# Modulation with stationary weights and two moving columns, most of it placed in slots of phase one

## The chip, the core and the metric
One NeuronCore of a Trainium2 chip. The time is that of the device for one execution, in microseconds (us). TensorE multiplies, VectorE and ScalarE work element by element, GpSimd builds masks, SyncE and ScalarE issue the transfers.

## What is computed
One step of a layer of a streaming encoder: 2048 prompt tokens and 64 sample tokens of width 1024, in float32. Cut to what the change touches:

```python
mod = jax.nn.silu(c) @ w_ada + b_ada              # c: (1, 1024), w_ada: (1024, 6144)
sh1, sc1, g1, sh2, sc2, g2 = jnp.split(mod[:, None, :], 6, axis=-1)
hn = rmsnorm(x, ln1_g) * (1.0 + sc1) + sh1
z = hn @ w_in                                     # four head groups read z
...
x = x + g1 * mix                                  # mix: concat of heads @ w_out
h2 = rmsnorm(x, ln2_g) * (1.0 + sc2) + sh2
x = x + g2 * (jnp.square(jax.nn.relu(h2 @ mlp_w1)) @ mlp_w2)
```

There are two vectors c, one for the prompt and one for the sample. Only sh1 and sc1 are needed before the input projection; the other four parts are read in the output projection and the MLP.

## The kernel before, in words
Three phases stand one after the other, each a block of its own with a join of all engines between them: `setup_phase` (the opening), `front_phase` (phase one: input projection and heads) and `tail_phase` (attention of later blocks, output projection, MLP). Features lie on the 128 partitions in KT = 8 tiles, tokens in the free dimension, in blocks of 512 (the first has the 64 sample tokens too, 576).

The opening computes the whole modulation in 12 chunks of 512 columns (NCH). For each, 2 MB of w_ada go into one of four `wada` buffers, issued by SyncE and ScalarE in turns. `chunk(c)` (L449 to L456) has c as the stationary side, 4 columns (`cful`, `chl`), and w_ada as the moving side: half of the depth in full float32, half as high and low parts, for which `halves_hi` (ScalarE, L272) and `halves_lo` (VectorE, L337) split the weights. The result is four rows in `pr`; `take_row` (L342) copies them, `turn_row` (L443) turns them into columns in `pm`, and `modulation(part)` on VectorE (L368 to L372) adds the bias and makes gs1 and gs2. Between the chunks lie the transposes of raw x (`turn("raw", f)`, stored to x_scratch), the squares and inverse roots, the transposes of normalised x (`xn`), which are evacuated into hT with scale gs1 and shift sh1 (L355), and the high and low parts hn_hi (L329) and hn_lo (L415).

Phase one walks slots. A block has 23 (SLOTS): slot 0 the low-rank strip, slots 1 to 22 one strip of 128 columns of w_in each. `strip(slot)` does 8 x 3 matmuls (high by high, low by high, high by low) for each column group of the block; block 0 has two groups of 288 columns. Its weights come by `load_weights` on SyncE (two slots ahead, into two buffers, after `w_lo_ok` of the strip two earlier), `weights_hi` on ScalarE (L864) and `weights_lo` on VectorE (L1089). Results go to a ring of four PSUM banks (`ring_no`, `bank_for`), which ScalarE empties in `ring_out`. Beside the strips a slot does the jobs that its number gives it (gates, norms, transposes, state updates, attention). The order on each engine is written out by hand in `step(slot)`; each engine works its list in order, so a wait in SyncE's list holds all its later loads and stores.

## Time and profile before
| | before |
|---|---|
| three plain runs, us | 2826.13, 2823.44, 2823.38 (median 2823.44) |
| the profiled execution, us | 2821.06 |
| its span, us | 2819.3 |
| TensorE busy | 96% (2718.6 us) |
| VectorE, ScalarE busy | 52%, 38% |
| moved | 485.99 MB, mean 172 GB/s |

The span runs from the first to the last instruction; the profiled execution has 1.8 us around it. Busy shares are means over phases with different limits, so they say what is scarce over the run and not what ends a stage.

### The profile page before, as it was taken

The page shows a single profiled execution, that of the slowest core. Times are in us where ns is not written, and L with a number is a line of the kernel's source. Part 1 is how long each engine was busy: PE and PEld are TensorE (multiplying, and loading weights), DVE is VectorE, ACT ScalarE, POOL GpSimd, SP SyncE. Part 2 cuts the span into 40 slices and gives each one's busy share as a digit, 9 for nine tenths or more (in the row PEclk, how much of TensorE's full clock was granted, in tenths as well). Part 3 has the DMA queues.
Part 4 walks back from the last instruction along what each step waited for, and adds up shares of the span by engine and source line. Part 5 has one row for each costly group of instructions (what it writes and reads, how often), then busy time and mean ns, then how long its engine had stood idle before and what let it go on. Part 6 is the DMA issues. An engine that isn't in the chain of part 4 may idle for free.

```text
span 2819.3 us, 36506 instructions
## 1 busy us (share of the span) xinstructions
PE 2718.6 (96%) x14669; PEld 2224.5 (79%) x14669; DVE 1459.5 (52%) x2315; ACT 1075.1 (38%) x1728; POOL 33.2 (1%) x43
## 2 busy tenths in 40 slices
PE   7999999999978999999999999999999999999996
PEld 2589777777766777777787878777777788999996
DVE  4455563554436657665564455555545434544553
ACT  3374846656434343433433322343222322221112
POOL 0000000000000000000000000001000000100000
PEclk9999999999989999999999999999999999999999
DMA  9533435324386676775435454534453643454441
GB/s 338 174 105 114 115 113 153 113 83 135 101 282 244 221 243 227 238 253 206 147 138 192 179 185 164 191 127 172 151 204 140 216 180 135 165 177 166 166 179 64
DMA packets 285934, 485.99 MB, mean 172 GB/s; under 512 B 21963, under 2 KB 168326, under 8 KB 285766
## 3 DMA queue, kind: packets, MB, share of 16 engines
q1 hardware_dynamic: 279526, 471.07, 48.7%
q10 hardware_dynamic: 6240, 12.58, 1.2%
q8 instruction: 118, 1.93, 0.3%
q14 instruction: 50, 0.41, 0.0%
HBM read 374.52 MB, written 109.06 MB: 172 GB/s over the span
## 4 chain that ended last, share of the span: by engine, by line
PE 62%; DVE 5%; ACT 2%; DMA 2%; issue 1%; SPq 1%; DVEq 0%; ACTq 0%
PE t_dn L2400 10%; PE t_dn L2404 10%; PE t_dn L2401 10%; PE t_dn L2442 7%; PE t_dn L2444 7%; PE t_dn L2443 7%; PE t_ob L2340 3%; PE t_sc L2317 2%; PE t_wt L2329 2%; DVE t_left L2137 1%; PE t_dn L2465 1%; PE t_dn L2467 1%; PE t_dn L2466 1%; DVE t_xs L2220 1%; DMA ring_lo<-lo_scratch 1%
## 5 line engine op out<-in xcount | busy, mean ns | idle before, releaser
L2400 PE MATMUL t_dn<-t_h_hi,ring_hi 128*128 128x512 f32 (+2 forms) x1600 | 588.0, 368 | 18.0 <-ACT t_h_hi L2027 7.1
L2220 DVE SCALAR_TENSOR_TENSOR t_xs<-t_dn,modT,t_xs 128x512 f32<-128x512 f32 (+2 forms) x768 | 422.5, 580 | 312.9 <-PE t_dn L2444 167.6
L2404 PE MATMUL t_dn<-t_h_lo,ring_hi 128*128 128x512 f32 (+2 forms) x1600 | 568.9, 356 | 3.8 <-DVE t_h_lo L2202 3.4
L2401 PE MATMUL t_dn<-t_h_hi,ring_lo 128*128 128x512 f32 (+2 forms) x1600 | 566.6, 354 | 0.0
L2442 PE MATMUL t_dn<-t_g_hi,t_w2h 128*128 128x512 f32 (+2 forms) x1120 | 412.3, 368 | 11.5 <-DVE t_xs L2220 9.3
L2444 PE MATMUL t_dn<-t_g_lo,t_w2h 128*128 128x512 f32 (+2 forms) x1120 | 396.6, 354 | 0.0
L2443 PE MATMUL t_dn<-t_g_hi,t_w2l 128*128 128x512 f32 (+2 forms) x1120 | 395.7, 353 | 0.0
L2252 DVE TENSOR_TENSOR t_rt<-t_rt 128x512 f32<-128x512 f32 (+2 forms) x160 | 95.8, 599 | 551.1 <-ACT t_g_hi L2076 551.1
L2400 PEld LDWEIGHTS t_dn<-t_h_hi,ring_hi 128*128 128x128 f32 x1600 | 304.2, 190 | 75.3 <-issue 32.1
L2404 PEld LDWEIGHTS t_dn<-t_h_lo,ring_hi 128*128 128x128 f32 x1600 | 303.3, 190 | 47.8 <-DVE t_h_lo L2202 6.9
L2401 PEld LDWEIGHTS t_dn<-t_h_hi,ring_lo 128*128 128x128 f32 x1600 | 304.5, 190 | 31.4 <-issue 0.5
L2074 ACT ACTIVATE t_rt<-t_dn 128x512 f32<-128x512 f32 (+2 forms) x160 | 83.7, 523 | 639.5 <-PE t_dn L2404 639.5
L1447 PE MATMUL f_zr<-hn_hi,ring_hi 128*128 128x512 f32 (+1 forms) x880 | 319.3, 363 | 6.5 <-ACT f_gb L897 2.6
L1449 PE MATMUL f_zr<-hn_hi,ring_lo 128*128 128x512 f32 (+1 forms) x880 | 309.9, 352 | 0.0
L1448 PE MATMUL f_zr<-hn_lo,ring_hi 128*128 128x512 f32 (+1 forms) x880 | 309.4, 352 | 0.0
L2442 PEld LDWEIGHTS t_dn<-t_g_hi,t_w2h 128*128 128x128 f32 x1120 | 211.9, 189 | 53.4 <-DVE t_xs L2220 20.6
L2444 PEld LDWEIGHTS t_dn<-t_g_lo,t_w2h 128*128 128x128 f32 x1120 | 211.7, 189 | 28.0
L1956 ACT ACTIVATE t_aT<-t_wt 128x512 f32<-128x512 f32 (+4 forms) x152 | 80.2, 528 | 398.9 <-PE t_wt L2329 398.8
L2443 PEld LDWEIGHTS t_dn<-t_g_hi,t_w2l 128*128 128x128 f32 x1120 | 212.3, 190 | 20.6
L1089 DVE TENSOR_TENSOR ring_lo<-f_wraw,ring_hi 128x1024 fp32r<-128x1024 f32 x90 | 110.1, 1224 | 215.8 <-ACT ring_hi L864 215.6
L1447 PEld LDWEIGHTS f_zr<-hn_hi,ring_hi 128*128 128x128 f32 x880 | 165.2, 188 | 39.4 <-issue 12.9
L864 ACT ACTIVATE ring_hi<-f_wraw 128x1024 fp32r<-128x1024 f32 x90 | 94.9, 1055 | 240.1 <-PE f_zr L1449 215.7
(344 smaller groups left out, 3426.1 us busy)
## 6 DMA issues: line engine op xcount, KB each, us to landing
ring_hi<-hi_scratch SPq DMA_DIRECT2D x120, 512.0 KB, 4.0
ring_lo<-lo_scratch SPq DMA_DIRECT2D x120, 512.0 KB, 4.9
t_w2h<-hi_scratch SPq DMA_DIRECT2D x96, 512.0 KB, 6.1
t_w2l<-lo_scratch SPq DMA_DIRECT2D x96, 512.0 KB, 7.1
f_wraw<-in_w_in_dram SPq DMA_DIRECT2D x88, 512.0 KB, 3.9
t_raw<-in_mlp_w_dram SPq DMA_DIRECT2D x64, 512.0 KB, 4.7
hi_scratch<-ring_hi SPq DMA_DIRECT2D x40, 512.0 KB, 5.6
lo_scratch<-ring_lo SPq DMA_DIRECT2D x40, 512.0 KB, 6.3
```

The source lines that it names most:

```text
L1089: dve.tensor_tensor(w_lo[n % 2][:, :, :], wraw[n % 2][:, :, :], w_hi[n % 2][:, :, :].bitcast(F32), ALU.subtract).then_inc(w_lo_ok, 1)
L1447: pe.matmul(out, wh, hi, start=(k == 0), stop=False)
L1448: pe.matmul(out, wh, lo, start=False, stop=False)
L1449: ins = pe.matmul(out, wl, hi, start=False, stop=(k == KT - 1))
L2220: ins = dve.scalar_tensor_tensor(out=cols, in0=dn[u % 4][:, s - a:t - a], scalar=modT[:, mod + f, m:m + 1], in1=cols, op0=ALU.mult, op1=AL ...
L2252: dve.tensor_tensor(r, r, r, ALU.mult).then_inc(g_sq, 1)
L2400: pe.matmul(out, hi[:, k, :], h_hi[:, k, a:e], start=(i == 0), stop=False)
L2401: pe.matmul(out, lo[:, k, :], h_hi[:, k, a:e], start=False, stop=False)
L2404: ins = pe.matmul(out, hi[:, k, :], h_lo[:, k, a:e], start=False, stop=(i == KT - 1))
L2442: pe.matmul(out[:, 0:e - a], hi[:, d, :], g_hi[c % 2][:, ft, a:e], start=(ft == 0), stop=False)
L2443: pe.matmul(out[:, 0:e - a], lo[:, d, :], g_hi[c % 2][:, ft, a:e], start=False, stop=False)
L2444: ins = pe.matmul(out[:, 0:e - a], hi[:, d, :], g_lo[c % 2][:, ft, a:e], start=False, stop=(ft == 1))
```

## The change
The opening computes only shift and scale of norm one, in 4 groups (PARTS) of 256 columns each of the two. Now the weights are the stationary side, 128x128 in float32 at a time, and the two vectors c are the moving side with 2 columns; results come out as columns on the partitions, so high and low parts, row copies and the small transposes are gone. The raw transposes of x stand ahead of the groups, the transposes of normalised x behind groups 1, 2 and 3, and the sample's in a PSUM bank of their own. Odd xn tiles are evacuated by ScalarE. All eight pieces of w_ada have buffers of their own and are loaded without waits; x comes first on ScalarE's queue in two halves. The opening also loads and splits the weights of strips 1 and 2 (EARLY).

The other 32 tiles of 128 columns are done in 16 groups of two, one at the end of each of slots 2 to 17 of phase one: SyncE loads two pieces of 512 KB into buffers not used yet (kst, oA, kq, tok), after TensorE is through with the group two earlier; TensorE does 2 x 8 matmuls with 2 columns into a bank of the ring; ScalarE adds the bias. VectorE makes gs2 in slot 20.

```diff
--- before.py
+++ after.py
...
 M_SH1, M_SC1, M_G1, M_SH2, M_SC2, M_G2 = 0, 8, 16, 24, 32, 40
+EARLY = 2
...
@@ -124,17 +125,14 @@
...
-    CT = CH // P
-    RING = 4
-    FIRST = 2 * D_MODEL // CH
-    HALF_K = KT // 2
+    PARTS = 4
+    PW = D_MODEL // PARTS
+    PF = KT // PARTS
     WIDE = BLK + DEC
 
...
@@ -149,47 +147,43 @@
...
+        wada = [[sb(f"wada{g}_{i}", [P, KT, PW]) for i in range(2)] for g in range(PARTS)]
+        early = [sb(f"early{n}", [P, KT, P]) for n in range(EARLY)]
...
+        def load_wada(eng, g, i):
+            col = (M_SH1, M_SC1)[i] * P + g * PW
+            eng.dma_start(wada[g][i][:, :, :], wa_v[:, :, col:col + PW]).then_inc(wada_in[g], 16)
...
@@ -206,30 +200,28 @@
...
-                    sp.dma_start(x_v[:, :, 0:BLK], raw[:, :, 0:BLK]).then_inc(raw_stored, 16)
-                    sp.dma_start(x_v[:, :, SEQ:SEQ + DEC], raw[:, :, BLK:WIDE]).then_inc(raw_stored, 16)
-
+            sp.dma_start(xsam[:, :], x_sample[0]).then_inc(xs_in, 16)
+            load_wada(sp, 0, 1)
+            load_rows(rows2, parts2, rows_in[1])
+            load_wada(sp, 1, 1)
+            for n in range(EARLY):
+                col = STRIPS_IN[n][2]
+                sp.dma_start(early[n][:, :, :], win_v[:, :, col:col + P]).then_inc(early_in, 16)
+            sp.dma_start(lra_raw[:, :].rearrange("p (k n) -> p k n", n=RANK), win_v[:, :, OFF_LRA:OFF_LRA + RANK]).then_inc(early_in, 16)
+            for g in range(2, PARTS):
+                load_wada(sp, g, 1)
+            for i in range(2):
+                sp.dma_start(mixc["wa2"][RANK * i:RANK * i + RANK, :], gla_wa2[0]).then_inc(blocks_in, 16)
+            sp.wait_ge(zeroed, 1)
+            for n in range(4):
+                for g, w in enumerate((rg_wa, rg_wx)):
+                    sp.dma_start(mixc["rgw"][64 * (n % 2):64 * (n % 2) + 64, g, n // 2,
+                                             64 * (n % 2):64 * (n % 2) + 64], w[0, n]).then_inc(blocks_in, 16)
+            for f in range(KT):
+                freed(sp, "raw", f)
+            freed(sp, "raws", 0)
+            sp.dma_start(x_v[:, :, 0:BLK], raw[:, :, 0:BLK]).then_inc(raw_stored, 16)
+            sp.dma_start(x_v[:, :, SEQ:SEQ + DEC], raw[:, :, BLK:WIDE]).then_inc(raw_stored, 16)
             sp.wait_ge(blocks_in, 16 * 10)
...
@@ -266,12 +257,9 @@
...
+            def early_halves(n):
+                act.wait_ge(early_in, 16 * (EARLY + 1))
+                act.activation(const["ring_hi"][:, n, :, :], early[n][:, :, :], ACT.Copy).then_inc(early_hi, 1)
...
@@ -283,24 +271,33 @@
...
-
-            for c in range(0, RING, 2):
-                load_wada(act, c)
+                    act.wait_ge(gs_ok, f // PF + 1)
...
+            def high(f):
+                freed(act, "xn", f)
+                act.wait_ge(s_ok, f + 1)
+                act.activation(hn_hi[:, f, :], hT[:, f, :], ACT.Copy).then_inc(hi_ok, 1)
+
+            for h in range(2):
+                act.dma_start(xrow[:, 2 * h:2 * h + 2, :], x_prompt[0, 2 * h * P:(2 * h + 2) * P, :].rearrange("(i p) n -> p i n", p=P)
+                              ).then_inc(x_in[h], 16)
+            for g in range(PARTS):
+                load_wada(act, g, 0)
...
@@ -309,37 +306,34 @@
...
+            for g in range(PARTS):
+                if g < EARLY:
+                    early_halves(g)
+                if g == 2:
+                    act.activation(mixc["lra_hl"][:, :, 0:RANK], lra_raw[:, :].rearrange("p (k n) -> p k n", n=RANK), ACT.Copy).then_inc(early_hi, 1)
+                    act.wait_ge(prm, 2)
+                    chain.link(act.activation(lam[:, 0, :], const["prm2"][:, R2_LAM:R2_LAM + 2], ACT.Abs))
+                    chain.link(act.activation(lam[:, 1, :], lam[:, 0, :], ACT.Exp, scale=-1.0))
+                    act.activation(lam[:, 2, :], lam[:, 1, :], ACT.Ln, bias=1.0).then_inc(lam_a, 1)
+                for f in range(g * PF + 1, (g + 1) * PF, 2):
+                    turned("xn", f)
+                for f in range(g * PF, (g + 1) * PF):
+                    high(f)
 
...
         def _(dve):
             chain = Chain(dve, dve_chain)
 
...
+            def early_rest(n):
+                dve.wait_ge(early_hi, n + 1)
+                dve.tensor_tensor(const["ring_lo"][:, n, :, :], early[n][:, :, :], const["ring_hi"][:, n, :, :].bitcast(F32), ALU.subtract)
+
+            def low(f):
+                dve.wait_ge(hi_ok, f + 1)
+                dve.tensor_tensor(hn_lo[:, f, :], hT[:, f, :], hn_hi[:, f, :].bitcast(F32), ALU.subtract)
 
...
@@ -351,70 +345,63 @@
...
+            def modulation(g):
+                dve.wait_ge(mod_full, g + 1)
+                a = g * PF
+                for i, m in enumerate((M_SH1, M_SC1)):
+                    out = modT[:, m + a:m + a + PF, :]
+                    ins = dve.tensor_tensor(out, pm[g % 2][:, i, :, :],
+                                            const["prm1"][:, R1_BADA + m + a:R1_BADA + m + a + PF].rearrange("p (f c) -> p f c", c=1)
+                                            .to_broadcast([P, PF, 2]), ALU.add)
+                    chain.link(ins)
+                ins = dve.scalar_tensor_tensor(
+                    out=gs1[:, a:a + PF, :], in0=modT[:, M_SC1 + a:M_SC1 + a + PF, :], scalar=1.0,
+                    in1=const["prm2"][:, R2_LN1 + a:R2_LN1 + a + PF].rearrange("p (f c) -> p f c", c=1).to_broadcast([P, PF, 2]),
+                    op0=ALU.add, op1=ALU.mult)
+                ins.then_inc(gs_ok, 1)
+                dve.wait_ge(gs_ok, g + 1)
+
+            def sample_columns(f):
+                dve.wait_ge(s_full, 1)
+                dve.tensor_scalar(hT[:, f, BLK:WIDE], ts[:, f, :], gs1[:, f, 1:2], modT[:, M_SH1 + f, 1:2],
+                                  ALU.mult, ALU.add).then_inc(s_ok, 1)
 
             turned("rows", 0)
-            dve.wait_ge(c_hi, 1)
...
+            for g in range(PARTS):
+                modulation(g)
+                for f in range(g * PF, (g + 1) * PF, 2):
+                    turned("xn", f)
+                for f in range(g * PF, (g + 1) * PF):
+                    sample_columns(f)
+                if g < EARLY:
+                    early_rest(g)
+                if g == 2:
+                    dve.wait_ge(early_hi, EARLY + 1)
                     dve.tensor_tensor(mixc["lra_hl"][:, :, RANK:], lra_raw[:, :].rearrange("p (k n) -> p k n", n=RANK),
                                       mixc["lra_hl"][:, :, 0:RANK].bitcast(F32), ALU.subtract)
-                if c == 4:
                     chain.link(dve.tensor_scalar(lam[:, 3, :], const["prm2"][:, R2_LAM:R2_LAM + 2], -1.0, 0.0,
...
@@ -436,53 +423,41 @@
...
-            def turn_row(c):
...
-            def chunk(c):
-                pe.wait_ge(wada_in[c % RING], 16 * (c // RING + 1))
-                wait(pe, row_read, c - 1)
-                for k in range(HALF_K):
-                    pe.matmul(pr[c % 2][:, :], cful[:, k, :], wada[c % RING][:, k, :], start=(k == 0), stop=False)
-                pe.wait_ge(wada_lo_ok, c + 1)
-                for k in range(HALF_K):
-                    pe.matmul(pr[c % 2][:, :], chl[:, HALF_K + k, :], wada_hi[c % 2][:, k, :], start=False, stop=False)
-                    ins = pe.matmul(pr[c % 2][:, :], chl[:, HALF_K + k, :], wada_lo[c % 2][:, k, :], start=False,
-                                    stop=(k == HALF_K - 1))
-                ins.then_inc(row_full, 1)
+            def modulation(g):
+                pe.wait_ge(wada_in[g], 32)
+                wait(pe, gs_ok, g - 1)
+                for i in range(2):
+                    for j in range(PF):
+                        for k in range(KT):
+                            ins = pe.matmul(pm[g % 2][:, i, j, :], wada[g][i][:, k, j * P:(j + 1) * P], cful[:, k, :],
+                                            start=(k == 0), stop=(k == KT - 1))
+                ins.then_inc(mod_full, 1)
...
             pe.wait_ge(masks, 2)
             turn("rows", 0)
+            pe.wait_ge(x_in[0], 16)
+            pe.wait_ge(x_in[1], 16)
+            for f in range(KT):
+                turn("raw", f)
+            pe.wait_ge(xs_in, 16)
+            turn("raws", 0)
+            turn("rows", 1)
             pe.wait_ge(silu_c, 1)
-            pe.wait_ge(c_lo, 1)
...
+            for g in range(2):
+                modulation(g)
+            pe.wait_ge(xn_ok, TPB + 1)
+            for k in range(KT):
+                ins = pe.transpose(ts[:, k, :], xsam[:, k * P:(k + 1) * P], ident[0:DEC, 0:DEC])
+            ins.then_inc(s_full, 1)
+            for f in range(2 * PF):
+                turn("xn", f)
+            for g in range(2, PARTS):
+                modulation(g)
+                for f in range(g * PF, (g + 1) * PF):
+                    turn("xn", f)
+
...
@@ -707,9 +693,16 @@
         def _(sp):
             def load_weights(slot):
                 n, i = weight_no(slot), slot % SLOTS
-                wait(sp, w_lo_ok, n - 1)
+                wait(sp, w_lo_ok, n - 1 - EARLY)
                 src, col = (wout_v, i * P) if slot >= NBLK * SLOTS else (win_v, STRIPS_IN[i - 1][2])
                 sp.dma_start(wraw[n % 2][:, :, :], src[:, :, col:col + P]).then_inc(w_in_sem[n % 2], 16)
+
+            def load_mods(g):
+                if g > 1:
+                    sp.wait_ge(z_full, ring_no["m", g - 2, 0] + 1)
+                for s in range(2):
+                    col = (16 + 2 * g + s) * P
+                    sp.dma_start(mod_w[g % 2][s], wada_v[:, :, col:col + P]).then_inc(mod_in[g % 2], 16)
 
...
@@ -754,8 +747,7 @@
             def load_kq(j):
                 sp.wait_ge(k_placed[0], 16)
                 sp.wait_ge(q_placed[0], 16)
-                if j:
-                    sp.wait_ge(z_full, ring_no["as", TPB - 1, 1] + 1)
+                sp.wait_ge(z_full, (ring_no["as", TPB - 1, 1] if j else ring_no["m", MODS - 1, 0]) + 1)
...
             def step(slot):
-                if slot and has_weights(slot + 2):
+                if slot > EARLY and has_weights(slot + 2):
                     load_weights(slot + 2)
+                if 2 <= slot < MODS:
+                    load_mods(slot)
...
@@ -816,8 +810,10 @@
...
-            load_weights(1)
-            load_weights(2)
+            load_weights(EARLY + 1)
+            load_weights(EARLY + 2)
+            load_mods(0)
+            load_mods(1)
             sp.wait_ge(init_ok, 1)
...
@@ -1020,6 +1016,14 @@
                 if kind == "nC" and j == 0:
                     norm_root(flows[0], "C")
 
+            def modulation(g):
+                bank = full("m", g, 0)
+                for s in range(2):
+                    m = 16 + 2 * g + s
+                    ins = act.activation(modT[:, m, :], bank[:, 2 * s:2 * s + 2], ACT.Identity,
+                                         bias=const["prm1"][:, R1_BADA + m:R1_BADA + m + 1])
+                ins.then_inc(z_free, 1)
+
...
@@ -1406,6 +1418,15 @@
                 if kind == "nC" and j == 0:
                     norm(flows[0], "C")
 
+            def modulation(g):
+                bank = bank_for("m", g, 0)
+                pe.wait_ge(mod_in[g % 2], 32 * (g // 2 + 1))
+                for s in range(2):
+                    for k in range(KT):
+                        ins = pe.matmul(bank[:, 2 * s:2 * s + 2], mod_w[g % 2][s][:, k, :], const["cful"][:, k, :],
+                                        start=(k == 0), stop=(k == KT - 1))
+                ins.then_inc(z_full, 1)
+
...
@@ -1429,8 +1450,8 @@
                 b, i = divmod(slot, SLOTS)
                 if i:
                     n = weight_no(slot)
-                    pe.wait_ge(w_hi_ok, n + 1)
-                    pe.wait_ge(w_lo_ok, n + 1)
+                    wait(pe, w_hi_ok, n + 1 - EARLY)
+                    wait(pe, w_lo_ok, n + 1 - EARLY)
```

## Rows read from the trace of the kernel before
**Rows 1.** Windows: length; busy us of PE, PEld, DVE, ACT, POOL; PEclk; DMA share; GB/s
```profile
0.00:10.00 10.00, 0.34 (x1) 0.18 (x1) 0.40 (x2) 3.02 (x4) 4.10 (x22) 1.00 0.82 287
10.00:20.00 10.00, 8.71 (x18) 1.64 (x19) 2.29 (x1) 3.55 (x2) 0.00 (x0) 1.00 1.04 392
...
50.00:60.00 10.00, 10.00 (x46) 3.80 (x45) 8.34 (x18) 3.83 (x2) 0.00 (x0) 1.00 1.04 385
...
90.00:105.60 15.60, 13.34 (x53) 3.88 (x51) 8.75 (x16) 1.91 (x1) 0.00 (x0) 1.00 0.00 0
```

**Rows 2.** Transfers of the opening, up to 105 us
```profile
DMA packets 17146, 30.22 MB, mean 288 GB/s; under 512 B 3091, under 2 KB 3254, under 8 KB 17142
```

**Rows 3.** Timeline, end of the opening: start us, us, engine, line
```profile
105.58 0.99 SPq L712 DMA_DIRECT2D f_wraw<-in_w_in_dram  x2
...
105.62 0.40 PE L1441 MATMUL f_zr<-hn_hi,lra_hl 128*32 128x288 f32 x1 [1.85 <-PEq L144]
...
111.10 0.29 PE L1441 MATMUL f_zr<-hn_hi,lra_hl 128*32 128x288 f32 x1
111.23 0.29 PE L1444 MATMUL f_zr<-hn_lo,lra_hl 128*32 128x288 f32 x1
113.20 0.37 PE L1447 MATMUL f_zr<-hn_hi,ring_hi 128*128 128x288 f32 x1 [1.67 <-DVE ring_lo L1089]
```

**Rows 4.** Timeline of TensorE, waits for ScalarE in phase one
```profile
198.36 0.37 PE L1447 MATMUL f_zr<-hn_hi,ring_hi 128*128 128x288 f32 x1 [2.14 <-ACT f_gb L897]
```

**Rows 5.** Transfers between 182 and 192 us, GB/s in 40 slices
```profile
GB/s 0 0 0 0 0 0 66 88 94 154 178 174 238 256 272 307 381 414 401 418 426 401 410 418 393 410 401 418 426 401 410 418 393 410 401 418 383 275 277 283
DMA packets 2434, 2.80 MB, mean 280 GB/s; under 512 B 32, under 2 KB 1410, under 8 KB 2434
...
x_scratch<-hT SPq DMA_DIRECT2D x1, 2048.0 KB, 8.8
```

**Rows 6.** Timeline of TensorE in the opening, modulation chunks
```profile
11.29 6.37 PE L451 MATMUL pr<-wada,cful 128*4 128x512 f32 x8 [4.20 <-DMA wada<-in_w_ada_dram]
...
19.52 3.60 PE L451 MATMUL pr<-wada,cful 128*4 128x512 f32 x8
...
24.99 0.41 PE L443 MATMUL pm<-ident,mod_rows 4*128 4x4 f32 x4
```

**Rows 7.** Timeline of TensorE in the tail, eight matmuls of attention
```profile
1510.66 0.40 PE L2404 MATMUL t_dn<-t_h_lo,ring_hi 128*128 128x512 f32 x1
1510.89 1.00 PE L2340 MATMUL t_ob<-t_vp,t_aT 128*128 128x64 f32 x8
1511.70 0.48 PE L2400 MATMUL t_dn<-t_h_hi,ring_hi 128*128 128x512 f32 x1
1512.02 0.39 PE L2401 MATMUL t_dn<-t_h_hi,ring_lo 128*128 128x512 f32 x1
```

**Rows 8.** TensorE groups by shape, whole run: busy us, mean ns
```profile
L2340 PEld LDWEIGHTS t_ob<-t_vp,t_aT 128*128 128x128 f32 x1008 | 135.2, 191 | 11.9
...
L443 PE MATMUL pm<-ident,mod_rows 4*128 4x4 f32 x48 | 4.9, 203 | 0.4 <-DVE mod_rows L342 0.4
```

**Rows 9.** Timeline of TensorE at the end, transposes
```profile
2797.05 1.94 PE L2484 MATMUL t_dn<-ident,t_xs 128*128 128x128 f32 x16 [2.68 <-DVE t_xs L2295]
...
2808.50 4.71 PE L2484 MATMUL t_dn<-ident,t_xs 128*128 128x128 f32 x24 [8.98 <-DVE t_xs L2295]
```

**Rows 10.** Groups of ScalarE and VectorE in the opening, 0 to 240 us
```profile
L279 ACT ACTIVATE hT<-strips 128x1024 f32<-128x1024 f32 x4 | 4.2, 1058 | 5.1 <-DMA strips<-in_x_prompt_dram 5.0
...
L355 DVE TENSOR_SCALAR hT<-tb,gs,modT 128x512 f32<-128x512 f32 x8 | 6.0, 805 | 0.5 <-PE tb L436 0.5
...
L329 ACT ACTIVATE hn_hi<-hT 128x576 fp32r<-128x576 f32 x8 | 4.7, 669 | 1.8 <-DVE hT L360 1.8
...
L415 DVE TENSOR_TENSOR hn_lo<-hT,hn_hi 128x576 fp32r<-128x576 f32 x8 | 5.6, 738 | 0.0
```

**Rows 11.** Timeline of ScalarE, its wait for strip weights
```profile
120.04 1.06 ACT L864 ACTIVATE ring_hi<-f_wraw 128x1024 fp32r<-128x1024 f32 x1 [6.16 <-DMA f_wraw<-in_w_in_dram]
```

More of the change, by code:

```diff
@@ L543, in front_phase, with mod_group @@
     RAW, XN, PAST_AT = (4, 7, 8, 9), (13, 14, 15, 17), SLOTS + 11
+    MODS = 16
+    def mod_group(slot):
+        return slot - 2 if 0 <= slot - 2 < MODS else None
     def tp_jobs(slot):
@@ L1041, in ring_out @@
                     attention_out(*job)
+                if mod_group(slot) is not None:
+                    modulation(mod_group(slot))
             def step(slot):
@@ L1046, in step @@
                     tokens_hi(b)
-                if has_weights(slot + 1):
+                if slot >= EARLY and has_weights(slot + 1):
                     weights_hi(slot + 1)
@@ L1289, in step @@
                     norm(flows[0], "C", oC, 4)
+                if slot == MODS + 4:
+                    dve.wait_ge(z_free, ring_no["m", MODS - 1, 0] + 1)
+                    for c in range(2):
+                        chain.link(dve.scalar_tensor_tensor(
+                            out=const["gs2"][:, :, c], in0=modT[:, M_SC2:M_SC2 + KT, c], scalar=1.0,
+                            in1=prm2[:, R2_LN2:R2_LN2 + KT], op0=ALU.add, op1=ALU.mult))
                 for f in at(slot, 18):
@@ L1469, in _ @@
                     attention(*job)
+                if mod_group(slot) is not None:
+                    modulation(mod_group(slot))
                 for job in tp_jobs(slot):
```

225 lines of the change are left out of this document (55 added, 170 removed).

## The prediction
> **What bounds the kernel now.** I read the page's slices first: TensorE is busy in 96% of the span and only the first slice stands out. So any stretch in which TensorE does other than strips is paid in full, and the opening is the stretch to look at. The windows of the opening [rows 1] show its two parts. Up to about 88 us the DMA engines are saturated at 385 to 392 GB/s (the reader should see the DMA share at 1.04 while TensorE has gaps); from 90 us the DMA share is 0.00 and TensorE is busy, so there the arithmetic of the modulation sets the end. The transfers are twelve pieces of 2 MB, 30.22 MB with all else by 105 us [rows 2]. Phase one starts at 105.6 us: SyncE asks for its first weights only then, slot 0 ends its matmuls at about 111.35 us, and slot 1 starts at 113.20 after waiting for the low half of its weights [rows 3]. From there TensorE is nearly gapless: in the sixteen slots after slot 1 its largest wait is 2.14 us [rows 4].
>
> **The sum is made against 2821.06 us**, the profiled execution (span 2819.3); the median of the plain runs is 2.4 us above it, inside what such runs differ by.
>
> **Part 1, the opening's transfers.** Shift and scale of norm one are 2048 columns, eight pieces of 1.05 MB: 8.4 MB in place of 25.2. With x (2.1), the sample rows (0.26), two early strips (1.05) and small things it is 12 MB of loads, then 2.4 MB of stores of raw x. At 385 GB/s from 2.5 us on, the loads have landed at 34 to 36 us and the stores at 40 to 42. Rows of 1 KB and 512 bytes aren't in the opening of before; the mix in [rows 5] (2.80 MB, half its packets under 2 KB) still moved at 380 to 426 GB/s once under way, so I add nothing. The transfers bound the opening's end at 42 us from below.
>
> **Part 2, the opening's matmuls.** Gone are 12 chunks: 8 full f32 matmuls of 512 columns, 3.60 us at the high clock, 6.37 for the first at the low one [rows 6], 8 on the high and low halves (1.9 us at 0.23 each, as the strip matmul in [rows 7]) and four small transposes each, some 70 us in all. In come 4 groups of 2 x 2 x 8 = 32 pairs of a 128x128 f32 load and a matmul of two columns. No such pair is in the trace. The nearest row is the attention's: eight f32 matmuls with a 128x128 stationary and 64 columns take from 1510.89 to 1511.70, 0.10 us each [rows 7]. Loads last 191 ns each [rows 8], so they overlap, and it is the load that sets the 0.10: 64 columns at the rate of [rows 6] would be 0.053. Fewer columns can't make that longer, so 0.105 is my value at the high clock. The lower bound is 0.07, from the 4x4 transposes of mod_rows (four in 0.41 us [rows 6], one of them 0.20 [rows 8]); the upper is 0.19, the load's own duration if nothing overlaps.
>
> The clock matters as much. At the low one the 24 transposes at the end of the run take 4.71 us against 1.94 for 16 at the high one, about 0.21 against 0.113 each until the clock rises among them [rows 9]. In [rows 6] the clock rose while full 512-column matmuls ran. In the new opening TensorE waits for x until some 10 to 13 us, does short bursts of transposes held up by their four banks, and then streams two columns per load. I take the low clock for the modulation groups: 0.21 x 32 = 6.7 us per group.
>
> The chain, with durations of [rows 10]: x is there at 10 to 13 us (2.1 MB ahead of all else on ScalarE's queue, at half to all of the rate). Then come five squares (1.2 with the read of the sum), the roots (about 1 us) and, because ScalarE must empty half of the banks, the transposes of raw x: group 0 starts at about 21. Groups 0 and 1 take it to 34.4; the sample's eight transposes and four xn turns at the low clock to 38.7; group 2 to 45.4; two turns 47.1; group 3 to 53.8. Behind it come its bias and scale (0.75), the last turn's transposes and evacuation (0.8), high halves (0.67 each) and the low halves of four tiles (0.74 each), 5.2 us, and 0.6 for the change of block: phase one starts at 59.6 instead of 105.6. I take 46.0 us off. The new order on SyncE's queue puts the eight small rgw loads and the raw stores behind the early strips; the stores land near 42 and are hidden by this chain, but would be the end themselves if the chain were faster than that.
>
> The Trainium skill speaks to both doubts. TensorE: Matmul & The Clock Gate, section LDWEIGHTS, gives P / 1.2 ns for a load of P columns, so 107 ns for 128, whatever the clock; the 0.10 of [rows 7] agrees with it, but no run here shows such a load at the low clock. If it held there, the groups would take 3.4 us each and the opening would be that of rival A. The same page, Part 4, says that transposes don't lift the clock; by [rows 9] they do here (only transposes run, and the later ones are fast), so the measurement decides, and the 24 transposes ahead of group 2 may lift it for a while.
>
> **Part 3, phase one starts with strips 1 and 2 ready.** Slot 1 no longer waits: 113.20 - 111.35 = 1.9 us off [rows 3]. The next loads have two slots to land: w3 and w4, four pieces of modulation weights (3.1 MB, 9 us) ahead of x of block 1 (2.1 MB). Group 0 is wanted at about 18 us after the start and x at 26, so these are hidden.
>
> **Part 4, sixteen slots with a group of 16 pairs each.** 16 x 0.105 = 1.68, and 0.09 for the first strip matmul behind it, which takes 0.32 to the next instead of 0.23 [rows 7]: 1.78 x 16 = 28.5 us, all on TensorE's path, at the high clock: each group is 1.7 us between strips of 6.4 (48 matmuls at 0.133, the pace that slot 0 has reached in [rows 3]), and the strip matmul behind the gap of 2.14 us in [rows 4] still lasts 0.37 us, as the one at 113.20 in [rows 3]. Bounds by pitch: 16 x 16 x 0.07 = 18 + 1.4, and 256 x 0.19 = 49 + 1.4. ScalarE's two tiny activations (0.23 each) go beside the strips. TensorE's old waits for ScalarE's evacuations, 2.14 at 198.36 [rows 4] and smaller ones, go under the longer slots: 3 us back.
>
> **Part 5, a new wait on SyncE.** From slot 2 to 15 SyncE waits for the end of group g - 2, that is for the end of the very slot, ahead of its next weight load and stores. Queued behind it: the load for slot s + 3, x_scratch (slot 11), oB (slot 12). A weight load then stands behind 1 MB of modulation weights: 1.57 MB in about 6.5 us, and ScalarE wants it 6.4 us later; at worst 0.5 us late, with over a slot left before TensorE needs it. At slot 11 the 2.1 MB of x_scratch (8.8 us to landing [rows 5]) stand in between too: the weights land some 12 us after the slot's end, ScalarE stands in its queue 5 us with the evacuations behind, and TensorE lacks a bank. 0 to 8 us; I take 3, because a longer slot eats half of it. ScalarE's wait for weights of 6.16 at 120.04 [rows 11] cost TensorE nothing when its banks were free.
>
> **Sum:** 2821.1 - 46.0 - 1.9 + 28.5 - 3 + 3 = 2801.7, less 2 for a clock that may rise among the transposes ahead of group 2: 2800.
>
> **Rivals.**
> A. The opening isn't bound by TensorE's clock: the small pairs count as activity, or a load keeps its 0.105 at the low clock. Groups 0 and 1 end at 27.7, the transposes at 30.3, group 2 at 33.7, group 3 waits for its weights (35.5) and ends at 39; phase one starts at 44.8. That is 15 us less: 2786. For it: [rows 6], in which the clock rose and stayed up over gaps of 2 us, and [rows 9]. Against: two columns against a load of 128 are hardly any streaming.
> B. SyncE's wait costs more than a bank now and then: in each of slots 6 to 13, where ScalarE was the one waited for, it is 2 us late: 16 instead of 3, 2813.
> C. Slower: a two-column matmul is too short to hide a load. Then the pair takes load plus matmul, 0.19 + 0.20 [rows 8]. The opening grows to 84 us, the slots to 256 x 0.39 = 100: 2821 - 21 - 2 + 101 = 2899. It decides from 384 p = 75, p = 0.195 us a pair, almost exactly the load's own duration. Against it: the 0.10 of [rows 7] with loads of the same size.
> D. The change saves no work in sum, only moves it: with the whole opening hidden behind transfers anyway there would be nothing to gain. The zero DMA share from 90 to 105.6 us and 25.2 MB against 8.4 [rows 1, 2] speak against it: 2821.
>
> **Chances.** Forecast 0.50, A 0.32, B 0.11, C 0.04, D 0.03. The forecast's own range, by the start of group 0 (18 to 24), part 5 and the pitch, is 2793 to 2809. The range of 8 in 10 takes in most of A and the nearer half of B: 2780 to 2814. Faster by over 0.2% (which is about what a measurement of this kernel can tell from no change): 0.93; within it 0.03; slower 0.04.
>
> **What would show it.** The granted clock between 20 and 54 us at its lower level and group rows of 6.7 us; if 3.4, A. First matmul of phase one at about 60 us. In slots 2 to 17 a group row of 1.7 us and strips still at 0.133 us a matmul. The bank wait, if any, at the start of slot 13 and released by ScalarE, whose own wait is for a DMA. The tail from 780 us of before on should be shifted and otherwise the same; a changed tail, or a phase one at the low clock, would make the prediction wrong in a way I haven't priced.

## The result, and the profile after

| kernel | median us | range us | ratio to before (95% interval) |
|---|---|---|---|
| before | 2823.4 | 2821.5 to 2826.1 | |
| after | 2904.4 | 2901.5 to 2907.5 | 1.0286 (1.0268 to 1.0304) |

The change makes the kernel 81 us slower. The forecast was 2800, with 2780 to 2814 as its range: it is wrong in sign and by 104 us. The span of the profiled execution is 2899.7, 80.4 more than before.

The page of after first, its busy times and two rows of its slices. The reader should see that TensorE is busy in 96% as before, and that in slices 2 to 5 (72 to 362 us) the granted clock is below 9, with hardly an idle tenth beside it: work at a lower speed, not waiting.

```profile
PE 2796.5 (96%) x15197; PEld 2356.4 (81%) x15197; DVE 1424.0 (49%) x2294; ACT 1062.5 (37%) x1751; POOL 33.1 (1%) x42
PE   6999999999997999999999999999999999999997
PEclk9787899999998999999999999999999999999999
```

The opening, from the timelines of ScalarE and of TensorE (start, duration, engine, line, operation; in brackets the idle time before it and its releaser):

```profile
0.73 0.97 ACTq L289 DMA_DIRECT2D strips<-in_x_prompt_dram  x2
1.73 16.52 ACTq L179 DMA_DIRECT2D wada<-in_w_ada_dram  x4
18.28 1.28 ACT L294 ACT_TABLE_LOAD   x1 [18.28 <-issue]
...
28.61 2.82 PE L423 MATMUL tb<-ident,strips 128*128 128x128 f32 x12 [13.55 <-ACT raw L276]
...
32.57 27.41 PE L432 MATMUL pm<-cful,wada 128*128 128x2 f32 x128
...
64.29 10.66 PE L432 MATMUL pm<-cful,wada 128*128 128x2 f32 x64
...
76.56 13.65 PE L432 MATMUL pm<-cful,wada 128*128 128x2 f32 x64
...
95.57 0.42 PE L1462 MATMUL f_zr<-hn_hi,lra_hl 128*32 128x288 f32 x1 [3.55 <-PEq L142]
```

Two things differ from the forecast's chain. ScalarE stands in the issuing of its four weight loads until 18.3, so its squares, its share of the raw turns and with them group 0 come at 32.57 and not at 21. And a group is 64 records, not 32: the two groups in the third row of TensorE are x128, 0.214 us each. Phase one starts at 95.57, 10.0 us before that of [rows 3], where the forecast had 46.0.

One reading needs care. Up to 64 us the profile of after shows a granted clock of 1.00, and its 0.214 us a pass doesn't fit that. e2_wide (below) has the same opening and the same 27.41 us for these 128 records, and there the clock between 33 and 60 us is 0.50. I read the low clock in both.

In phase one the start of the strip of slot 1 (first row of L1468 in the timeline) is at 101.0, 12.2 earlier than in [rows 3]; that of slot 18 is at 335.53 against 249.67, 85.9 later. So slots 1 to 17, with the sixteen groups among them, took 98.1 us longer. Windows of both kernels between 130 and 280 us (width, TensorE busy and instructions, granted clock, DMA share, GB/s), before, whose slot 18 starts at 249.67, and then after:

```profile
130.00:160.00 30.00, 30.00 (x212) 1.00 0.28 75
160.00:190.00 30.00, 29.83 (x219) 1.00 0.39 118
190.00:220.00 30.00, 27.39 (x206) 1.00 0.36 107
220.00:250.00 30.00, 29.01 (x226) 1.00 0.20 53
```

```profile
130.00:160.00 30.00, 30.00 (x186) 0.78 0.41 112
160.00:190.00 30.00, 30.00 (x197) 0.83 0.53 144
190.00:220.00 30.00, 29.61 (x217) 0.94 0.43 115
220.00:250.00 30.00, 25.37 (x166) 0.80 0.56 175
250.00:280.00 30.00, 27.95 (x148) 0.63 0.43 123
```

The same in single rows of TensorE's timeline, from the group in slot 3 into the next strip. Ahead of it the strip runs at 0.13 to 0.14 us a matmul, as in [rows 3]; behind it at 0.24, until the clock comes back:

```profile
126.17 0.29 PE L1469 MATMUL f_zr<-hn_lo,ring_hi 128*128 128x288 f32 x1
126.30 0.30 PE L1470 MATMUL f_zr<-hn_hi,ring_lo 128*128 128x288 f32 x1
126.44 0.73 PE L1426 MATMUL f_zr<-cful,f_kq 128*128 128x2 f32 x6
...
129.29 1.63 PE L1426 MATMUL f_zr<-cful,f_tok 128*128 128x2 f32 x7
130.78 0.59 PE L1468 MATMUL f_zr<-hn_hi,ring_hi 128*128 128x288 f32 x1
131.16 0.44 PE L1469 MATMUL f_zr<-hn_lo,ring_hi 128*128 128x288 f32 x1
131.41 0.44 PE L1470 MATMUL f_zr<-hn_hi,ring_lo 128*128 128x288 f32 x1
```

And the one long gap, in slot 12, ahead of its group: SyncE's queue, ScalarE, TensorE. SyncE issues the next modulation weights at 238.12, when the group of slot 11 has ended; the store of raw x (2 MB) and then the weights of slot 14's strip stand behind them. ScalarE waits 12.11 us for these weights with its evacuations behind, TensorE 5.57 for a bank:

```profile
238.12 0.37 SPq L705 DMA_DIRECT2D f_kq<-in_w_ada_dram  x1
238.53 0.58 SPq L705 DMA_DIRECT2D f_tok<-in_w_ada_dram  x1
239.22 0.82 SPq L718 DMA_DIRECT2D x_scratch<-hT  x1
240.08 2.94 SPq L698 DMA_DIRECT2D f_wraw<-in_w_in_dram  x1
...
250.65 1.06 ACT L860 ACTIVATE ring_hi<-f_wraw 128x1024 fp32r<-128x1024 f32 x1 [12.11 <-DMA f_wraw<-in_w_in_dram]
...
252.05 3.57 PE L1426 MATMUL f_zr<-cful,f_kst 128*128 128x2 f32 x16 [5.57 <-ACT f_gb L893]
```

How the 98 us divide, by the timelines: the sixteen groups last 66.5 together (from a group's first row to the first row of what follows); the strips of slots 3 to 17 last 118.7 in place of 15 x 6.6 = 99, which is 20 for the low clock; about 12 are left, 8.2 of them waits of the groups for banks that ScalarE frees. Of the 66.5, 16 x 3.4 = 54 would be there at the high clock.

### The profile page after: what moved, and what is told of

Its sections match the earlier page's. It is cut to its first block, busy times and chain, and to the rows that moved or that the text cites. A ratio compares the mean times of both kernels' runs of the same rounds, so it can differ in the third digit from the quotient of the medians.

```text
span 2899.7 us, 37608 instructions
## 1 busy us (share of the span) xinstructions
PE 2796.5 (96%) x15197; PEld 2356.4 (81%) x15197; DVE 1424.0 (49%) x2294; ACT 1062.5 (37%) x1751; POOL 33.1 (1%) x42
## 4 chain that ended last, share of the span: by engine, by line
PE 61%; DVE 5%; ACT 2%; issue 1%; DMA 1%; SPq 0%; DVEq 0%; ACTq 0%
PE t_dn L2423 10%; PE t_dn L2427 10%; PE t_dn L2424 10%; PE t_dn L2465 7%; PE t_dn L2467 6%; PE t_dn L2466 6%; PE t_ob L2363 3%; PE t_sc L2340 2%; PE t_wt L2352 2%; DVE t_left L2160 1%; PE t_dn L2488 1%; PE t_dn L2489 1%; PE t_dn L2490 1%; DVE t_xs L2243 1%; DVE t_taken L2165 1%
## 5 line engine op out<-in xcount | busy, mean ns | idle before, releaser
L1468 PE MATMUL f_zr<-hn_hi,ring_hi 128*128 128x512 f32 (+1 forms) x880 | 329.3, 374 | 1.3 <-issue 1.1
L1469 PE MATMUL f_zr<-hn_lo,ring_hi 128*128 128x512 f32 (+1 forms) x880 | 318.2, 362 | 0.0
L1470 PE MATMUL f_zr<-hn_hi,ring_lo 128*128 128x512 f32 (+1 forms) x880 | 318.1, 361 | 0.0
L1468 PEld LDWEIGHTS f_zr<-hn_hi,ring_hi 128*128 128x128 f32 x880 | 174.8, 199 | 33.5 <-issue 12.9
```

Of the source, the lines that this page charges most:

```text
L1468: pe.matmul(out, wh, hi, start=(k == 0), stop=False)
L1469: pe.matmul(out, wh, lo, start=False, stop=False)
L1470: ins = pe.matmul(out, wl, hi, start=False, stop=(k == KT - 1))
```

## The experiments

Theory, formed on these rows. (a) A row of a matmul record in the trace isn't a matmul: an f32 matmul stands there twice, as two passes with a load of 128 columns each, at 0.105 us a pass at the high clock and 0.213 at the low one. So a slot's group is 3.4 us, not 1.7. (b) These passes stream two columns each; behind such a stretch the granted clock is mostly at its low level, and the next strip pays. (c) The opening lost its start to ScalarE's queue. (d) SyncE's wait costs a bank in slot 12. Rivals: the waits and transfers alone, without (a) and (b); and a pair that is load plus matmul in series, 0.39 us, my rival C, whose 2899 looks like a hit.

### What the slots' matmuls cost: e1_few, e3_single

e1_few:

```diff
-                    for k in range(KT):
+                    for k in range(1):
```

> Each slot's group keeps its transfers, its waits and its place, but only the first of the eight contraction steps of each column group is computed (2 of 16 matmuls), so gate one and shift, scale and gate two come out wrong. The changed kernel is at 2904.4. Theory (each f32 matmul is two load passes of 0.105 us, so a group is 32 x 0.105 = 3.4 us; and the run of nearly empty matmuls lets TensorE's clock fall, which costs another 2 to 3 us a slot on the strips): 28 of 32 passes gone is 16 x 28 x 0.105 = 47 us, the clock stays at its high level in slots 2 to 17 and gives some 40 back: 2817, 2808 to 2826. Rival W (the slots grew by waits: SyncE's wait for the group's end, transfers behind it, ScalarE late with banks; the matmuls cost only what was forecast, 1.78 a slot): 16 x 1.56 = 25 less, 2880. Rival S (a matmul of two columns hides nothing of its load, 16 x 0.39 a group, and the low clock has another cause): 14 x 16 x 0.39 = 87 less as well, but the strips would keep their slow stretches.

Measured 2825.0 (ratio 1.0007, 0.9998 to 1.0017): 79 less than after, where the theory had 87 and rival W 24. So nearly all of the loss hangs on these 224 matmuls: 448 passes at 0.107 are 48 us of it. Most of the rest is the clock: one of the strips of slots 3 to 17 lasts over 7 us here, and in after fourteen of the fifteen do.

e3_single:

```diff
-  ins = pe.matmul(bank[...], mod_w[g % 2][s][:, k, :], const["cful"][:, k, :],
+  ins = pe.matmul(bank[...], hn_hi[:, k, s * P:s * P + P], hn_hi[:, k, 2 * P:2 * P + 2],
```

> The slots' 16 matmuls take fp32r operands that lie there already (high halves of the tokens, 128 columns stationary, 2 moving) in place of the f32 weights and the vector; the transfers, waits and places stay, gate one and shift, scale and gate two come out wrong. Theory (an f32 matmul is two passes with a load each, an fp32r one is one pass): 16 records a group in place of 32, 1.7 us in place of 3.4, 27 us less; the empty stretch is half as long, so that the clock falls later or less, 0 to 40 more: 2904 - 27 - 20 = 2857, 2835 to 2880. Rival (the two records are one matmul's halves, and the pass costs what its weights cost, whatever the type): 32 records or 16 of twice the length, 2904. Rival S (load and matmul in series, 0.39 a pair): no less than 16 x 0.39 a group, 2904.

Measured 2853.2 (1.0107, 1.0090 to 1.0124), 51 less. The records settle (a). The slots compute 16 x 16 = 256 matmuls in both kernels. Summary of the line (shortest, median and longest in ns; first and last start), for one of the four weight tiles of after (64 matmuls each), and then in e3_single, where all 256 read one tile:

```profile
L1426 PEld LDWEIGHTS f_zr<-cful,f_kst x128: 186/192/333, 114.9 to 315.1; 128*128 128x128 f32 x128
L1426 PE MATMUL f_zr<-cful,f_kst x128: 165/251/372, 114.9 to 315.1; 128*128 128x2 f32 x128
```

```profile
L1426 PEld LDWEIGHTS f_zr<-hn_hi x256: 186/192/333, 116.0 to 284.3; 128*128 128x128 f32 x128
L1426 PE MATMUL f_zr<-hn_hi x256: 164/250/372, 116.0 to 284.3; 128*128 128x2 f32 x128
```

64 matmuls are 128 records in f32; 256 are 256 in fp32r. Load (192) and matmul (251 and 250) last the same in both, and a group lasts 3.49 us in after and 1.70 in e3_single where the clock is high: 0.107 us a pass. So a load does hide behind its neighbours, and rival C's price of 0.39 a pair in series is wrong though its total was near. 27 of the 51 us are the 256 passes that are gone. The other 24 are mostly clock: six of the fifteen strips of slots 3 to 17 last over 7 us, where in after fourteen do.

### What brings the clock down: e2_wide, e4_spread

e2_wide:

```diff
-  ins = pe.matmul(bank[:, 2 * s:2 * s + 2], mod_w[g % 2][s][:, k, :], const["cful"][:, k, :],
+  ins = pe.matmul(bank[:, 64 * s:64 * s + 64].rearrange("p (a c) -> p a c", c=2), mod_w[g % 2][s][:, k, :],
+                  const["cful"][:, k, :].rearrange("p (a c) -> p a c", a=1).to_broadcast([P, 32, 2]),
```

> The slots' groups compute the same thing with the two moving columns repeated 32 times, 64 columns in place of 2; result and everything else as in the changed kernel (2904.4). Theory: the load sets the pace at 0.105 as before, as with the attention's 64-column matmuls in the tail, so a group still takes 3.4 us, but the columns that stream count as work for the clock: it stays high in slots 2 to 17, some 35 to 40 us less, 2867, 2855 to 2880. Rival L (it is the loads, or the waits in between, that bring the clock down, not the lack of columns): no change, 2900 to 2908. Rival P (more streaming costs more time: 64 columns at the low clock outlast the load): slower, 2910 to 2930.

Measured 2876.2 (1.0191, 1.0176 to 1.0206), 28 less, inside the theory's range and short of its middle. A group still takes 3.5 us with 32 times the columns, and the clock, in the same windows as above:

```profile
130.00:160.00 30.00, 29.86 (x219) 1.00 0.59 158
160.00:190.00 30.00, 29.31 (x238) 1.00 0.49 131
190.00:220.00 30.00, 27.51 (x213) 1.00 0.50 133
220.00:250.00 30.00, 24.37 (x133) 0.66 0.46 150
250.00:280.00 30.00, 30.00 (x241) 1.00 0.55 149
```

The one low window here is that of the bank waits ahead of the groups of slots 11 and 12 (2.5 and 5.6 us), which are still there. A third fall, at 293.8 us, stands behind a wait of 1.1 us. Over slots 1 to 17 the granted clock is 0.94, in after 0.82. The loads are the same in number and size, and only the columns changed: rival L falls.

e4_spread moves the same matmuls, two columns wide, in between the strip's own; their bank is opened between the strip's two:

```diff
+    if g and mod_group(slot) is not None:
+        modulation(mod_group(slot), k)
     pe.matmul(out, wh, hi, start=(k == 0), stop=False)
...
-    if mod_group(slot) is not None:
-        modulation(mod_group(slot))
```

> The 16 matmuls of a group are no longer one run at the end of the slot: two of them stand ahead of each of the eight contraction steps of the strip's second column group (0.42 us of loads, then three matmuls of 288 columns, 0.40), with their bank opened between the strip's two. Same work, same result. Theory: the same 3.4 us a group, but no stretch without streaming is longer than 0.42 us, so the clock stays high: 35 to 40 us less, 2867, 2855 to 2885 (a bank that ScalarE frees late may cost a few us). Rival L (the clock goes by the share of loads over a slot, or by something else in phase one): falls as before, 2900 to 2910. Rival I (each change between f32 and fp32r, or between a small and a large matmul, costs about 0.1 us): 16 changes a slot in place of 2, 16 x 14 x 0.1 = 22 back, 2885 to 2895 at the high clock.

Measured 2868.2 (1.0159, 1.0144 to 1.0174), 36 less. Two matmuls (four passes) and three of the strip repeat every 0.85 us, against 0.40 for the strip's three alone: 0.45 for four passes, 3.6 us a slot, as much as in one run. Rival I's 0.1 for each change isn't there. The granted clock over slots 1 to 17 is 0.96. Two edits of different kinds, more columns or shorter stretches, thus bring the clock back, which carries (b).

### The opening and the queues: e5_onsync, e6_late, e7_wide_both

e5_onsync takes the four loads off ScalarE's queue and puts each on SyncE's ahead of its partner:

```diff
-            for g in range(PARTS):
-                load_wada(act, g, 0)
...
+            load_wada(sp, 0, 0)
             load_wada(sp, 0, 1)
```

> Only the opening's queues change: the four pieces of modulation weights that ScalarE issues go to SyncE's queue, each ahead of its partner; ScalarE issues x alone. Changed kernel 2904.4. Theory (ScalarE's first arithmetic came at 18.3 us only because it stood in the issuing of these four loads for 16.5 us, and TensorE waited 13.6 us for its banks): squares start when x is there, near 10 us, group 0 starts 8 to 12 us earlier, phase one near 86 in place of 95.6: 2894, 2889 to 2898. Rival (all in one queue the weights land later than before, and group 0 waits for its own 2 MB or group 1 for the next): no gain or a few us lost, 2900 to 2910. Slots 2 to 17 as they were in both.

Measured 2886.3 (1.0219, 1.0203 to 1.0234), 18 less, more than the 6 to 15 expected. The mechanism is right: ScalarE's first square is at 8.90 and not at 21.10, group 0 starts at 20.18 in place of 32.57, slot 1 at 89.8 in place of 101.0. That is the 11 of (c). In the trace 8.4 more lie in slots 1 to 17, where nothing was edited: 226.1 us in place of 234.5, of which the strips of slots 3 to 17 have 3.3 (115.4 for 118.7). In which slots it falls differs from one execution to the next (the four plain runs of after have a mean clock of 0.961 to 0.973); why it was kinder here I leave open.

e6_late:

```diff
-                if 2 <= slot < MODS:
-                    load_mods(slot)
                 b = block_at(slot, XN[3] + 1 - SLOTS, 0)
...
                     store_tok(f, "v")
+                if 2 <= slot < MODS:
+                    load_mods(slot)
```

> Only SyncE's order in the slots changes: the two loads of modulation weights, with the wait for the end of the group, stand behind the slot's stores in place of ahead of them. Theory (the store of raw x and then the strip's weights stood behind that wait, so that the weights of slot 13 landed 12 us late and TensorE waited 5.6 us for a bank between slots 12 and 13): the store goes out earlier, some 4 to 8 us less, 2898, 2895 to 2902. Rival (what is late is the traffic itself, 2.1 MB of store with the modulation's 1 MB beside it, in whatever order): no change, 2902 to 2907.

Measured 2894.5 (1.0261, 1.0239 to 1.0283), 10 less, where 4 to 8 were expected. The time alone doesn't carry this: the interval overlaps that of after, and one of the four runs took 2906.6, as long as after. The trace does. The waits of TensorE (line waited for: us in total, times, longest), between 100 and 330 us, in after and then in e6_late:

```profile
PE f_zr L1426 <- ACT f_gb L893: 6.7, 2, 5.6
```

```profile
PE f_zr L1426 <- ACT f_gb L893: 2.2, 2, 1.1
```

The store of raw x is issued at 226.93 in place of 239.22, and the long wait is gone. So the queue's order was its cause, not the traffic. That is 4.5 us; the strips of slots 3 to 17 have 2.6 more (116.1 for 118.7), and what else there is may be the same spread as in e5_onsync.

e7_wide_both is e2_wide with the same 64 columns in the opening's groups:

> As e2_wide (64 streamed columns in the slots' groups), and the same in the opening's four groups. e2_wide is at 2876.2. Theory: with streamed columns the clock rises in the opening as well, 256 passes at 0.105 in place of 0.21 for most of them: phase one starts 20 to 25 us earlier, near 73; 2853, 2848 to 2860. Rival (at the low clock the opening's pace is the load's and the clock doesn't rise from load-bound work): no change from e2_wide, 2873 to 2880.

Measured 2860.6 (1.0142, 1.0111 to 1.0173), 16 less than e2_wide by the medians; its four runs stand in two pairs, 2852.4 and 2852.6, 2868.7 and 2868.9, and the profiled one is of the faster pair. The trace has the theory's 20 to 25 and a little more. Groups 0 and 1, then 2, then 3, in e2_wide and in e7_wide_both:

```profile
32.87 27.41 PE L432 MATMUL pm<-cful,wada 128*128 128x2 f32 x128
64.73 10.55 PE L432 MATMUL pm<-cful,wada 128*128 128x2 f32 x64
76.88 13.65 PE L432 MATMUL pm<-cful,wada 128*128 128x2 f32 x64
```

```profile
32.41 14.45 PE L432 MATMUL pm<-cful,wada 128*128 128x64 f32 x128
49.23 7.26 PE L432 MATMUL pm<-cful,wada 128*128 128x64 f32 x64
57.20 7.26 PE L432 MATMUL pm<-cful,wada 128*128 128x64 f32 x64
```

51.6 us of groups become 29.0, and phase one starts at 69.4 in place of 95.9. The slower pair wasn't traced; e9_all_few below has a trace of an opening that 64 columns did not keep fast, which would account for such a pair.

### All together, and the price of each half: e8_all, e9_all_few, e10_narrow, e11_block

e8_all has the four edits in one kernel: 64 columns in opening and slots, groups spread over the strip, the loads on SyncE's queue, the modulation weights behind the stores.

> All four edits together with the group spread over the strip as in e4_spread: 64 streamed columns in opening and slots, ScalarE's weight loads on SyncE's queue, modulation weights behind the stores. From e4_spread's 2868.2: opening 20 to 25 for the clock and 8 to 10 for the queue, 4 to 8 for the order of the stores. Theory: the terms add, 2868 - 22 - 9 - 5 = 2832, 2824 to 2842, still not under the 2822.6 of the kernel before, because 16 groups of 3.4 us (54 us) are more than the opening gives. Rival (the transfers bound the opening, landed at 42 us, so queue and clock don't add): 2845. Rival (spread and wide together lose what one alone gave): 2850 or more.

Measured 2829.0 (1.0021, 1.0012 to 1.0031). Its opening, in TensorE's timeline:

```profile
11.12 4.33 PE L424 MATMUL tb<-ident,strips 128*128 128x128 f32 x20 [4.31 <-DMA strips<-in_x_prompt_dram]
16.21 1.53 PE L424 MATMUL tb<-ident,strips 128*128 128x128 f32 x12 [0.76 <-ACT raw L279]
...
19.05 14.48 PE L433 MATMUL pm<-cful,wada 128*128 128x64 f32 x128
...
56.04 0.37 PE L1467 MATMUL f_zr<-hn_hi,lra_hl 128*32 128x288 f32 x1 [4.03 <-PEq L142]
```

Again 0.113 a pass; phase one starts at 56.0, 49.6 us before that of [rows 3]. So the gain that I had forecast for the opening (46.0) can be had, and is taken back in the slots. The ten runs lie between 2825.9 and 2830.3.

e9_all_few is e8_all with the first contraction step alone in the slots, as e1_few was of after:

> e8_all with only the first contraction step of each column group in the slots (2 of 16 matmuls; gate one and shift, scale and gate two come out wrong). It prices the two halves of the change apart: what the short opening gives and what the slots take back. e8_all is at 2829.0 and its phase one starts at 56.0, 49.6 us earlier than that of the kernel before. Theory (what the slots cost is the count of load passes and nothing else): 16 x 28 x 0.105 to 0.113 = 47 to 51 less: 2780, 2775 to 2786, so the opening alone is worth 42 to 45. Rival (ScalarE's extra evacuations, SyncE's waits and the 8 MB of transfers cost phase one something of their own): less comes back, 2790 to 2805.

Measured 2781.0 (0.9846, 0.9829 to 0.9862), 48.0 below e8_all, where 16 x 28 passes at 0.107 are 47.9. Without that work the kernel is 41.6 us faster than before.

Its six runs stand in two groups: four from 2778.1 to 2782.0, and two at 2793.4 and 2793.7, of which the first is the profiled one. The code of its opening is that of e8_all, the trace isn't:

```profile
19.36 25.63 PE L433 MATMUL pm<-cful,wada 128*128 128x64 f32 x128
49.11 7.26 PE L433 MATMUL pm<-cful,wada 128*128 128x64 f32 x64
57.09 7.26 PE L433 MATMUL pm<-cful,wada 128*128 128x64 f32 x64
```

Groups 0 and 1 take 25.6 us for the 14.5 of e8_all, at a granted clock of 0.54 between 20 and 50 us for 1.00 there, and phase one starts at 69.3, 13.2 later. So 64 columns kept the high clock in e8_all, and here they ran for some 23 us at the low one before it came back. The clock fell at 21.5 us, 2 us into the groups; why here and not in e8_all is open. By the four faster runs alone (median 2779.1) the slots' work costs 49.9.

The sum 49.6 off in the opening, 16 x 32 x 0.107 = 54.8 on in the slots gives 5.2, near the 6.2 measured for e8_all beside the kernel before (2829.0 and 2822.8). The traces show that this is partly luck. Slot 1 of e8_all starts 51.4 earlier than in [rows 3] (61.79), slots 1 to 17 last 64.0 longer (200.4 for 136.5), and the stretch behind them is 4.6 shorter, mostly for a reason that the section on the prediction gives (the tail). Of the 64.0, the passes are 54.8. The other 9 are two strips at the low clock (11.4 us each for 9.9), waits for banks, and 3.6 us for a slot's passes between the strip's matmuls, where 32 at 0.107 are 3.4.

e10_narrow is e8_all with two columns in the slots, e11_block e8_all with the groups in one run at the slot's end:

> e8_all with the slots' matmuls at two moving columns again (the opening's keep 64). Theory (spread over the strip, a group leaves no stretch without streaming, so the width no longer matters): 2829, 2825 to 2833. Rival (both are needed: with two columns the average streaming of a slot is still too little): the clock falls in some slots, 2836 to 2850.

Measured 2829.7 (1.0025, 1.0015 to 1.0034).

> e8_all with the slots' groups in one run at the end of the slot again, 64 columns wide. In e2_wide the clock still fell in three of sixteen slots, where TensorE had stood waiting for a bank. Theory (wide is as good as spread except behind waits, and the stores' order has taken most of these away): 2831, 2827 to 2840. Rival (the spread does something of its own, such as hiding the loads behind the strip's long matmuls): 2842 to 2850.

Measured 2831.6 (1.0031, 1.0016 to 1.0046). Both are inside their theory's range, and either of the two edits is enough to keep most of the clock: over slots 1 to 17 it is 0.98 in e8_all, 0.97 in e10_narrow and 0.96 in e11_block. Falls are left in slots 11 to 13, beside waits for banks that are left too (2.2 and 1.1 us ahead of the groups in e11_block), and one in slot 3 of e10_narrow. No kernel that does all the work is faster than the kernel before; e8_all and e10_narrow come within 0.3% of it.

A version that beats both would need fewer passes for the late two thirds of the modulation, such as the form of before (the weights moving, in high and low halves of fp32r). It wasn't tried, and whether its extra tiles fit beside those of phase one isn't shown.

## Why the prediction was wrong, step by step

By the profiled executions the miss is 101 us: 36 in the opening (phase one at 95.6, forecast 59.6) and 70 in slots 1 to 17 (98.1 longer, forecast 28.5), of which about 5 come back in the tail.

**What bounds the kernel, and part 1.** Right in what matters: the last transfers of the opening landed near 47 us, a little behind the 40 to 42 forecast, while groups 0 and 1 were still running, and no part of the result comes from them.

**Part 2, the pairs.** This is the step that failed. "Eight f32 matmuls with a 128x128 stationary and 64 columns take from 1510.89 to 1511.70, 0.10 us each": the eight records of [rows 7] were four matmuls. The line's loop in the code (two heads times two tiles) says four, and the same can be seen in [rows 6], where HALF_K = 4 matmuls of a chunk stand as x8, which I also called eight. The 0.105 was right, for a pass. With 2 passes a matmul the opening's groups are 4 x 64 x 0.213 = 54.5 at the low clock in place of 27; the trace has 27.4 + 10.7 + 13.7 = 51.7. That is +25 on the forecast, and the same count is +26 in the slots.

**Part 2, the clock.** Right that the low clock would hold in the opening with two columns a load (0.50 in e2_wide between 33 and 60 us, 0.54 in after between 65 and 95). By the Trainium skill (TensorE: Matmul & The Clock Gate, section LDWEIGHTS) a load of 128 columns takes 107 ns, a figure without the clock in it; the passes at 0.107 at the high clock agree, the 0.214 of 32.57 to 59.9 doesn't, so the measurement decides. Rival A, in which the opening wasn't bound by the clock, is refuted for two columns. With 64 its clock is there in e8_all and not in the traced run of e9_all_few.

**Part 2, the chain.** Start of group 0: 21 forecast, 32.6 measured. I priced x's landing, squares, roots and banks, and left out that ScalarE issues four more loads of 1 MB first, and stands in them until 18.3. The prediction listed what the new order does on SyncE's queue and not on ScalarE's. 11 us, by e5_onsync.

**Part 3.** Right: slot 1 starts without a wait.

**Part 4.** 28.5 forecast. The same count makes it 54; and "at the high clock: each group is 1.7 us between strips of 6.4" fell with it. The argument was made from idle gaps of 2 us, which had not brought the clock down; the group is 3.4 us of passes with two columns each, and it did. Some 32 us of the 98 (12 in the groups, 20 in the strips). I had put the low clock into the opening for that very reason and not asked it of the slots. At "a phase one at the low clock, would make the prediction wrong in a way I haven't priced" the text named the case and should have priced it.

**Part 5.** The mechanism and the releasers are as forecast (weights some 12 us after the end of slot 11, ScalarE 12.1 us in its queue for them where I had said 5, TensorE without a bank), the place is the group of slot 12 and not the start of slot 13. 3 was taken from a range of 0 to 8; the wait is 5.6, and 4.5 us of waiting went with the new order (e6_late).

**Rivals.** C's total of 2899 came from a serial pair (0.39), and e3_single shows no such thing: 0.107 a pass in an unbroken stream, twice a matmul, plus the clock. It did hold the right question, where the loss begins, "from 384 p = 75, p = 0.195": the true p is 0.213, and 384 x 0.213 = 82 lies on the slower side. It got 4 in 100 because I set the 0.10 of [rows 7] against it, the very number that hung on the false count.

**Back in the tail.** Slot 18 is 85.9 us late, the end 80.4. The last rows of the tail's loops are 81.0 late, its first 86.5; about 5 us come back between. Most of that is a clock that fell in before and not in after: around 2372 and 2492 us of before the windows 2360:2390 and 2485:2500 show 0.94 and 0.89, those of after for the same work (2446:2476 and 2570:2585) 1.00, and the delay of after shrinks there by 1.9 and 2.7. Another 2 go near 800 us. Why the clock fell in before is open; it isn't a gain of the change.

## What to carry to other kernels

Divide before you price: take a line whose number of matmuls the code gives, and compare it with the records that the trace has for it; f32 counts double. Weights as the stationary side with two moving columns cost here one pass of 0.107 us at the high clock for each 128 x 128 load (two passes, 0.213, for f32), as much as with 64. Behind a run of such passes the clock was low for whoever came next. Spreading them between long matmuls, or widening them at no cost in passes, kept most of it in the slots; in the opening widening kept it in one trace and not in another, so look at the clock of several executions. And list, for each engine, all that it issues ahead of its first piece of arithmetic.

## What the runs showed of the hardware

- An f32 matmul with 128 x 128 weights and two columns is two load and matmul records, 0.21 us at the high clock (3.49 us for 16 in a slot of after), 0.43 at the low one (27.41 us for 64 in its opening); an fp32r one is one record, 0.107 (1.70 us for 16 in e3_single).
- 64 moving columns take as long as 2 behind such a load in the slots (3.5 us a group for both).
- Behind 32 passes of two columns, strips met the low clock (0.24 us a matmul for 0.13; fourteen of fifteen strips in after last over 7 us). With 64 columns three did (e2_wide), all beside waits for banks. In pieces of four passes the clock over the slots was 0.96 (e4_spread), for 0.82.
- 64 columns did not bring a low clock back in the opening of the traced run of e9_all_few: 128 passes took 25.6 us, where e8_all's took 14.5 at the high one.
- Four loads of 1 MB on ScalarE's queue, behind 2 MB of x, kept ScalarE from any arithmetic for 16.5 us.
